# Two-block layer on one core: latent attention with scores two iterations in front, branch splits inside the merge projection, slot comparisons in the routing, sixteen raw expert buffers

## What is computed

```python
q, k, v = _mla_qkv(p, ...)           # 8 heads, 96 query/key channels, 64 value channels
attn_lat = softmax(q @ [k, kc].T) @ [v, vc]       # 1024 queries, 1024 + 256 keys, per head
four_lat = fft2(p_f).real                         # (1024, 512)
x = x + g1 * ((sig(ga) * (attn_lat @ w_o_attn) + sig(gb) * (four_lat @ w_fourier)) @ w_out)
h2 = modulate(rms(x, norm2_g), sh2, sc2)
aff = softmax(h2 @ w_router)                      # 16 experts
gate, idx = top_k(aff.T, 128)                     # each expert takes its 128 best tokens
ye = (silu(h2[idx] @ w_g) * (h2[idx] @ w_u)) @ w_d * gate    # 1024 -> 512 -> 1024
out = x + g2 * scatter_add(ye, idx)
```

## Time and profile before

| | us |
|---|---|
| median of 3 runs | 3254.71 (3249.96 to 3255.36) |
| the profiled execution, its own time | 3252.33 |
| its span, first to last instruction | 3250.2 |
| TensorE busy | 2822.3 (87%) |
| VectorE busy | 1540.8 (47%) |
| ScalarE busy | 1080.6 (33%) |
| latent loop, first scores to last output | 2278 to 2598 |
| second merge projection, its splits and its products | 2598 to 2706 |
| routing, top-k | 2840 to 2898 |
| experts | 2906 to 3250 |

### The profile page before, as it was taken

The page is one execution under the profiler, slowest core; times in us unless marked ns, Lnnn a source line. Parts: engine busy times, 40 slices in busy tenths (PEclk is TensorE's granted clock), DMA queues, the critical chain, the costliest instruction groups (busy, mean ns, idle before and its releaser), DMA issues. The chain is left out here.

```text
span 3250.2 us, 40600 instructions
## 1 busy us (share of the span) xinstructions
PE 2822.3 (87%) x16494; PEld 2301.4 (71%) x16494; DVE 1540.8 (47%) x2184; ACT 1080.6 (33%) x1888; POOL 295.0 (9%) x304
## 2 busy tenths in 40 slices
PE   5999998998998988982987999987899988919997
PEld 3777777776777887881775888746777876817776
DVE  3225544333625314236534121025666653589997
ACT  4213311111215214141235111114555521207776
POOL 0004400000100000000000000003000010101333
PEclk9999999999999998995988899998999999859999
DMA  6554641220301112017423112111000054229998
GB/s 175 187 184 139 197 137 55 68 74 34 117 24 56 52 42 63 14 39 210 130 91 112 27 49 91 49 64 48 1 1 1 3 179 124 110 86 340 368 380 275
DMA packets 272229, 357.43 MB, mean 110 GB/s; under 512 B 54988, under 2 KB 185060, under 8 KB 270381
## 3 DMA queue, kind: packets, MB, share of 16 engines
q1 hardware_dynamic: 228908, 214.15, 20.6%
q0 software_dynamic: 31616, 119.71, 11.4%
q10 hardware_dynamic: 11520, 20.98, 1.8%
HBM read 282.70 MB, written 76.80 MB: 111 GB/s over the span
## 5 line engine op out<-in xcount | busy, mean ns | idle before, releaser
L225 PE MATMUL ps<-h_hi,st_w_lo 128*128 128x512 f32 x592 | 249.0, 421 | 15.9 <-PEq L828 10.1
L222 DVE TENSOR_TENSOR ew_lo<-wraw,ew_hi 128x1024 fp32r<-128x1024 f32 x192 | 247.0, 1338 | 18.3 <-ACT ew_hi L219 17.2
L222 DVE TENSOR_TENSOR w_lo<-wraw,w_hi 128x1024 fp32r<-128x1024 f32 (+2 forms) x116 | 120.0, 1053 | 276.5 <-ACT w_hi L219 275.8
L227 PE MATMUL ps<-h_hi,st_w_hi 128*128 128x512 f32 x592 | 234.3, 396 | 0.0
L226 PE MATMUL ps<-h_lo,st_w_hi 128*128 128x512 f32 x592 | 233.1, 394 | 0.0
L219 ACT ACTIVATE ew_hi<-wraw 128x1024 fp32r<-128x1024 f32 x192 | 197.3, 1060 | 56.3 <-DMA wraw<-w_e_up 44.6
L219 ACT ACTIVATE w_hi<-wraw 128x1024 fp32r<-128x1024 f32 (+2 forms) x116 | 104.0, 917 | 292.7 <-PE ps L227 165.6
L225 PE MATMUL ps<-w_hi,merged_lo 128*128 128x512 f32 (+2 forms) x408 | 161.5, 396 | 37.4 <-DVE w_lo L222 31.2
L225 PE MATMUL ps<-h_hi,w_lo 128*128 128x512 f32 x384 | 156.6, 408 | 19.1 <-DVE w_lo L222 19.1
L225 PE MATMUL ps<-merged_hi,w_lo 128*128 128x512 f32 x400 | 160.5, 401 | 9.8 <-DVE w_lo L222 9.8
L226 PE MATMUL ps<-merged_lo,w_hi 128*128 128x512 f32 x400 | 159.8, 400 | 0.0
(11 more groups left out here) (495 smaller groups left out, 6462.3 us busy)
## 6 DMA issues: line engine op xcount, KB each, us to landing
wraw<-w_in SPq DMA_DIRECT2D x98, 512.0 KB, 4.9
wraw<-w_e_gate SPq DMA_DIRECT2D x64, 512.0 KB, 8.7
wraw<-w_e_up SPq DMA_DIRECT2D x64, 512.0 KB, 7.9
wraw<-w_e_down SPq DMA_DIRECT2D x64, 512.0 KB, 9.9
mod_w<-w_mod POOLq DMA_DIRECT2D x12, 2048.0 KB, 9.5
gates<-st_zo ACTq DMA_DIRECT2D x48, 256.0 KB, 2.0
rw_in<-rw_scan POOLq DMA_DIRECT2D x8, 1280.0 KB, 6.0
mg_gates<-gates POOLq DMA_DIRECT2D x16, 512.0 KB, 4.8
```

Source lines behind the costliest of these rows:

```text
L222: return dve.tensor_tensor(dst, src, hi.bitcast(F32), ALU.subtract)
L225: pe.matmul(out, a[1], b[0], start=first, stop=False)
L227: return pe.matmul(out, a[0], b[0], start=False, stop=last)
```

## The change

1. Latent loop: TensorE works on scores(n+2) in iteration n, with its first chunk ahead of transpose group 2 and its two others at the iteration's end. VectorE does row_max(n+2) after the copy of group 1 and after output, ahead of the head piece's low part. The wait for the head piece's low part moves from ahead of group 0 to ahead of group 1. Head pieces stand at iterations 0, 2, 3, 4, 6, 7, 8, 10, 11, 12 of 16, where they stood at 2 to 11.
2. Merge projection: the block of splits is gone; the attention chunks are split at the front of the `gemm`, the Fourier chunks after the splits of the first three weight pieces. Fourier chunks are loaded on POOL into two buffers, and the gate loads wait for the attention splits.
3. Routing: `BATCH = (2, 8, 12, NE)`; comparisons 2 to 8 and the second batch of indices are in the routing block.
4. Experts: 16 raw buffers, all filled during routing, and ring=8 split buffers.
5. Semaphores `mod_` and `norm_` are retired too after the first merge.

```diff
+            if side is not None and "second" in side:
+                order.append(("second", 0))
...
                 def gate_loads(gp, ev):
+                    if raw is not None:
+                        raw["in"](gp, 0)
                     for m in range(KD):
+                        if m == 2 and raw is not None:
+                            raw["in"](gp, 1)
...
+                    ready = [[("m2_lo", n)] if raw is not None and m == 0 else None for n in (4, 8)]
...
-            retire("rw_", "st_", "gn_", "at_", "cm_")
+            retire("rw_", "st_", "gn_", "at_", "cm_", "mod_", "norm_")
...
+                HEAD_AT = (0, 2, 3, 4, 6, 7, 8, 10, 11, 12)
...
                     for n in range(N):
-                        if n + 1 < N:
-                            scores(n + 1)
                         pe.wait_ge(S("ml_e"), n + 1)
                         if n:
                             pe.wait_ge(S("ml_pa"), 2 * n)
                             pe.wait_ge(S("ml_pd"), n)
+                        transposes(n, 0)
                         if n and next_head(n - 1):
                             hh, i = next_head(n - 1)
                             pe.wait_ge(S("ml_hlo"), 5 * hh + i + 1)
-                        transposes(n, 0)
                         transposes(n, 1)
                         if n >= 2 and n % 2 == 0:
                             output(n // 2 - 1)
+                        if n + 2 < N:
+                            scores(n + 2, 0)
                         pe.wait_ge(S("ml_pa"), 2 * n + 1)
                         transposes(n, 2)
                         if next_head(n):
                             pe.wait_ge(S("ml_pd"), n + 1)
                             head(*next_head(n))
+                        if n + 2 < N:
+                            scores(n + 2, 1)
+                            scores(n + 2, 2)
...
                     row_max(0)
+                    row_max(1)
                     for n in range(N):
-                        if n + 1 < N:
-                            row_max(n + 1)
...
                             output(n // 2 - 1)
+                        if n + 2 < N:
+                            row_max(n + 2)
                         if next_head(n):
                             head(*next_head(n))
...
+                def four_in(gp, i):
+                    for c in (2 * i, 2 * i + 1):
+                        if i:
+                            gp.wait_ge(S("m2_lo"), c + 3)
+                        gp.dma_start(fr[:, c % 2, :], four_d[:, c, :]).then_inc(S(f"m2_in{c}"), 16)
+                    if not i:
+                        gp.wait_ge(S("m2_lo"), 4)
...
+            wraw2 = sb(moe, "wraw2", [P, 12, SPLIT])
+            own = dict(raw=[wraw[:, i, :] for i in range(4)] + [wraw2[:, i, :] for i in range(12)],
+                       w=pair(moe, "ew", [P, 8, SPLIT]), loaded=16, split=0, base=used["gemm_hi"])
...
-            BATCH = (2, 10, NE)
+            BATCH = (2, 8, 12, NE)
...
-                gemm(jobs, ring=12, banks=5, pool=rows_io, own=own,
+                gemm(jobs, ring=8, banks=5, pool=rows_io, own=own,
```

More of the change, by code:

```diff
@@ L382, in _ @@
                                 view(whi[:, n % ring, :], n)).then_inc(S("gemm_lo"), 1)
+                        elif what == "second":
+                            side["second"]("dve", dve)
                         else:
@@ new lines, in second, with split @@
+                fr = sb(st, "four_raw", [P, 2, T])
+                def split(kind, eng, chunks):
+                    for n in chunks:
+                        src, dst, c = (ao[:, n, :], oa, n) if n < 4 else (fr[:, n % 2, :], of, n - 4)
+                        if kind == "act":
+                            if n >= 4:
+                                eng.wait_ge(S(f"m2_in{n - 4}"), 16)
+                            high(eng, dst[0][:, c, :], src).then_inc(S("m2_hi"), 1)
+                        if kind == "dve":
+                            eng.wait_ge(S("m2_hi"), n + 1)
+                            low(eng, dst[1][:, c, :], src, dst[0][:, c, :]).then_inc(S("m2_lo"), 1)
@@ L2788, in second @@
             moe = ExitStack()
-            wraw2 = sb(moe, "wraw2", [P, 4, SPLIT])
-            own = dict(raw=[w[:, i, :] for w in (wraw, wraw2) for i in range(4)], w=pair(moe, "ew", [P, 12, SPLIT]),
-                       loaded=8, split=0, base=used["gemm_hi"])
-            first_pieces = [piece for name in ("gate", "up")
-                            for piece in pieces_of(A[f"w_e_{name}_2"][0, 0].rearrange("(p k) f -> p k f", p=P), "N")]
+            wraw2 = sb(moe, "wraw2", [P, 12, SPLIT])
+            own = dict(raw=[wraw[:, i, :] for i in range(4)] + [wraw2[:, i, :] for i in range(12)],
+                       w=pair(moe, "ew", [P, 8, SPLIT]), loaded=16, split=0, base=used["gemm_hi"])
+            first_weights = ([A[f"w_e_{name}_2"][0, e].rearrange("(p k) f -> p k f", p=P) for e in range(2)
+                              for name in ("gate", "up")])
+            first_down = [A["w_e_down_2"][0, 0].rearrange("(k p) n -> p k n", p=P)[:, :, c * 512:(c + 1) * 512]
+                          for c in range(2)]
+            first_pieces = [piece for w in first_weights + first_down for piece in pieces_of(w, "N")][0:16]
             def own_loads(sp):
@@ L2858, in _ @@
                     tr.then_inc(S("ro_st"), 1)
-                    for e in range(BATCH[0]):
+                    for e in range(BATCH[1]):
                         slot_sums(pe, e)
@@ L2911, in _ @@
                     indices(dve, link, 0)
+                    for e in range(BATCH[0], BATCH[1]):
+                        onehot(dve, e)
+                    indices(dve, link, 1)
+                    onehot(dve, BATCH[1])
                 @block.gpsimd
```

79 lines of the change are left out of this document (29 added, 50 removed).

## The result

| | us |
|---|---|
| changed kernel, median of 20 runs | 3258.01 (3251.72 to 3263.99) |
| kernel before, median of 20 runs beside them | 3249.56 (3236.32 to 3255.36, and one run of 3702.35) |
| ratio, 95% interval | 1.0033 (1.0023 to 1.0043) |
| profiled execution of the changed kernel, and its span | 3258.35, 3256.5 |

The change makes the kernel slower by 0.33% (by the two medians 0.26%); the one run of 3702 us is left out of the ratio. The forecast was 3261, in a range of 3240 to 3278. The span went from 3250.2 to 3256.5, +6.3 where +6 was forecast. But the terms are not all those of the forecast: two are wrong, and one is missing.

A forecast was written before the change was run, and what follows sets the result against it. TensorE was taken to bound the latent loop; in the experts TensorE, VectorE and DMA were within a tenth of each other. Loop +26, merge -2, experts with their start -18 gave +6: 3261 us, range 3240 to 3278.

The forecast's parts named there:

- The loop's stall: Latent loop: TensorE waits 1.66 us for a head piece's low part in 30 iterations, +49; old waits removed, -27.
- The 5.6 us for a second first product: Latent loop: a first scores product behind transposes costs 0.09 us more, now paid twice per iteration, 62 times: +5.6.
- Merge projection: Second merge projection: attention products start some 6 us earlier, first Fourier product moves; taken as -2, range -5 to +2.
- six loads of 0.52 MB from 2604.2 take 8.2 us: Merge projection: at 385 GB/s the last Fourier loads end at 2612.4, first Fourier product at 2616, -2.7.
- the forecast's other bound: Merge projection: if a load takes 7.6 us as the gates did, the first Fourier product comes at 2618.1, -0.5.
- The clock's +2: Merge projection: TensorE stands about 4 us and may come back at the lower clock, the +2 end of the range.
- Rival 4: Merge projection: POOL's loads are held up by the port rule, +4 on any case; chance 0.25 within the others.
- the rule: Merge projection: GpSimd can't write a DMA's descriptors while VectorE holds their shared port pair; stage +2 rather than -2.
- Routing: Routing and start of experts: first low part about 14 us after first indices rather than 21, -7; otherwise -2.
- Stream: Expert stream: 16 pieces loaded during top-k rather than 8 take loads out of the stream; -11, range -4 to -16.
- rival 2: Experts run at TensorE's period: -16 in the stream, up to 4 us more at the start, 3252; chance 0.2.
- Rival 1: Experts: the ring of 8 binds, periods stay at 19.3 and only the start is gained: +17, 3272; chance 0.2.

The follow-up runs named there:

- the variants: Three runs of the kernel before with the merge change alone: last Fourier loads ahead of gate loads, on ScalarE's queue, or chunks split earlier; 1.0002, 1.0003, 1.0011.
- e_nomult: Kernel before with both expert parts alone, and without GpSimd's multiplication of each expert's result by the residual gate: 0.9916 of the kernel before, 3223.1 us.
- e_tail: Kernel before with both expert parts alone, splits of the last two weight pieces moved behind the last activations' low part: 0.9943 of the kernel before.
- e_r10: Kernel before with both expert parts alone, but 12 raw buffers and a ring of 10 rather than 16 and 8: 0.9946 of the kernel before.
- m_first: Kernel before with the merge change alone, POOL issuing the loads of Fourier chunks 2 and 3 ahead of all gate loads: 1.0002 of the kernel before.

## Why the prediction was right in sum, and where it was wrong

**The loop's stall: right in mechanism and place, its terms mis-sized.** The wait was summed at 1.66 us and is 1.67 by the weight loads, 30 times. What TensorE lost is the matmuls' own wait, 42.9 us in all, not 49: the sum ended where weights are loaded again, but a weight load's wait begins while the transposes before it still run. The other side was mis-sized likewise: the old waits, as TensorE's matmuls have them, are 24.7 us in all, and the changed loop still has 5.4 of others, so 19 came back, not 27. The largest of the old ones, kernel before:

```profile
PE ps L2471 <- DVE mla_pT L2610: 10.8, 15, 0.8
PE ps L2489 <- ACT mla_pT L2546: 8.3, 33, 0.3
```

The 5.6 us for a second first product can't be found: TensorE's busy time fell from 293.8 to 291.3. So +23.6 of idle and -2.5 of busy, 21, against 27.6. Errors of the same kind stood on both sides and took each other off in part.

**Merge projection: wrong.** The step that failed is "six loads of 0.52 MB from 2604.2 take 8.2 us". First, POOL issued the last loads 3.4 us later than worked out (14.7 rather than 11.3 us after the last output product for the last of them), since ScalarE waited 4 us for weight pieces 1 and 2, which came in beside the Fourier chunks. Second, the forecast's other bound, 7.6 us for a load from the gates' row, was the right one; the bytes that it was weighed against left out the weight pieces, some 1.8 MB over this stretch. That the bytes set the time is argued (see the variants). The two loads took 7.3 and 7.5 us. With both, 2618.1 + 3.4 - 2597.0 = 24.5 us, and 24.6 was measured. The clock's +2, named for a pause of 4 us, was paid for one of 9.5. Third, "from 2624.1 on the stage is TensorE's and stays as it is" failed too: the wait for the x rows behind it is 3.6 us shorter, for a reason that no run shows, and the net price of the merge change in the traces is +1.2 us.

**Rival 4 did not come true.** At 2628.70 POOL issued a load in 0.53 us while VectorE's low parts of two SBUF operands ran from 2627.18 to 2629.54. The prediction had stretched the rule: the Trainium skill (SBUF — State Buffer, Who interferes with whom) ties the hold on descriptor writing to VectorE's two-port modes, and says of an operation with two SBUF inputs that it contends with GpSimd's reads. Both agree with the rows: the issue here was not held, and GpSimd's multiplication, which reads SBUF, lengthens low parts (e_nomult). The merge itself comes out near the rival's +4 by another way.

**Routing: right,** 13.8 us where 14 was forecast, and no second gap at the change of block (2.93 us for ScalarE). Two comparisons moved into a stream that VectorE bounds take 2.2 back. The forecast had named them there and priced them at nothing.

**Stream: right in direction.** ScalarE's waits for weights are gone. Two terms are off: -6.65 within it rather than -11, with -4.4 at its start, which was named in rival 2 alone. Together they are the forecast's -11, by luck. What came late next was VectorE, as named, and TensorE half a microsecond behind it (e_nomult), so the far end of -16 was out of reach; only without the multiplication does the stream come near it (288.8 to 273.3). Rival 1, that the ring of 8 binds, is wrong for the stream (idle ahead of low parts 2.9 us) but right for its end: +5.35, which no step of the forecast looked at. The rival's "1.34 us where undisturbed ones take 1.14" set a length against a distance of starts; by lengths it is 1.34 against 1.22.

**The sum** of the two traces was met within 1 us, by luck in good part: a loop 5 too dear, a merge 7 too cheap, an end of 5 not seen, 3.6 given back at a load that the forecast took as fixed, and 2.5 us of the size that executions differ by. The parts, timed alone, give 1.0077, 1.0004 and 0.9934, together 1.0015 with some 0.0024 to either side; the whole has 1.0033. The best of the complete versions is the kernel before with the expert parts alone, 3228.5 us, 0.9934; e_tail and e_r10 can't be told from it. The retired semaphores were never timed by themselves.

## What to carry to other kernels

When a loop is pipelined one stage deeper, ask of each small step that shares a buffer with the main work which producer it now stands behind: here 0.74 us of VectorE's work, moved behind one row maximum, stopped TensorE for 1.4 us on average, thirty times. When a shorter ring frees memory, read the order at both ends of the stream, not only in its middle. And before a load is split into pieces that wait for each other's buffer, add up all bytes that will be in flight beside the last piece, those of other queues too. And follow a stretch's loss to the next wait for a load before you book it: here most of 4.8 us was gone by the first indices.

## What the runs showed that was not expected

- A load of 512 KB took 6.8 to 9.3 us from issue to use with some 6 MB moving around it (the last two Fourier chunks, six traces), and its place on POOL's or ScalarE's queue changed that by 1 us at most, save for one that had one weight piece beside it when it was issued (4.3 us, m_first).
- The 4 MB load of x rows, issued 80 us behind the changed stretch, took 18.7 to 22.8 us in the six traces with the merge change and 22.6 to 26.1 us in the eight without.
- GpSimd's 16 multiplications of two SBUF operands, 3.2 us each in the changed kernel, go with 27 us more on VectorE over 192 low parts, 1.36 rather than 1.22 us each.
- TensorE, VectorE and the loads can stand so close that taking 27 us of work off the one at the bound gave 8 us.
